# A one-layer hybrid decoder block: max8 rounds spread over the expert loop, and the work of the tail dealt out anew between ACT, DVE, POOL and PE

## What is computed

```python
x = x + merged @ w_o[l]
x = x + moe(rms_norm(x, g_ffn[l]), ...)          # 64 SwiGLU experts, top 8, one shared expert
ple_gate = jax.nn.sigmoid(rms_norm(x, g_ple_in[l]) @ w_ple_gate[l])
x = x + ple_gate * rms_norm(p[l] @ w_ple_proj[l], g_ple_out[l])
```

## Time and profile before

| | |
|---|---|
| median of three executions | 1212.77 us (1207.9 to 1215.7) |
| the profiled execution | 1205.96 us, span 1204.2 us |
| mean granted clock of TensorE in it | 0.989 of full |
| busy: PE, DVE, ACT, POOL | 1142.6 (95%), 840.2 (70%), 771.5 (64%), 398.4 us (33%) |
| bytes moved | 291.52 MB, mean 242 GB/s |
| expert loop, last matmul at | about 1127.8 us |
| projections of `p` | 1133.5 to 1149.4 us |
| gate matmuls | 1152.8 to 1199.6 us |

### The profile page before, as it was taken

How to read it: one execution, slowest core, us unless ns; L and a number is a source line. 1 busy time by engine, 2 the same in 40 slices (tenths; PEclk the granted TensorE clock), 3 DMA queues, 4 the chain that set the end, 5 groups by cost and what they waited for, 6 DMA issues and landing times. The chain is left out here.

```text
span 1204.2 us, 17716 instructions
## 1 busy us (share of the span) xinstructions
PE 1142.6 (95%) x5403; PEld 909.9 (76%) x5403; DVE 840.2 (70%) x1199; ACT 771.5 (64%) x1266; POOL 398.4 (33%) x475
## 2 busy tenths in 40 slices
PE   6999999998999999899999999999999999999898
PEld 5988888697566775688888887777877887777566
DVE  6336432377344336799999998888889998888574
ACT  6534433276233221688888888878888888888471
POOL 1110000042355000155555554445445544453200
PEclk9999999999799999999999999999999999999899
DMA  6312312024001247699999999999999999999611
GB/s 231 141 70 95 114 70 90 20 59 154 37 1 39 102 193 317 238 363 393 384 384 381 382 385 386 357 365 370 355 364 365 364 386 370 368 380 297 189 71 53
DMA packets 71804, 291.52 MB, mean 242 GB/s; under 512 B 15123, under 2 KB 20278, under 8 KB 46806
## 3 DMA queue, kind: packets, MB, share of 16 engines
q1 hardware_dynamic: 52422, 254.15, 54.2%
q0 software_dynamic: 18768, 34.79, 11.4%
q10 hardware_dynamic: 576, 2.10, 0.4%
HBM read 284.61 MB, written 42.07 MB: 271 GB/s over the span
## 5 line engine op out<-in xcount | busy, mean ns | idle before, releaser
L1342 DVE TENSOR_TENSOR arena_r<-arena,win_r 128x1024 fp32r<-128x1024 f32 x256 | 296.5, 1220 | 58.4 <-ACT win_r L905 54.4
L905 ACT ACTIVATE win_r<-arena 128x1024 fp32r<-128x1024 f32 x256 | 250.1, 1056 | 57.5 <-DMA arena<-in_w_exp_up 54.8
L1707 PE MATMUL bank<-win_r,work_r 128*128 128x512 f32 x512 | 206.1, 403 | 21.0 <-DVE x_low_r L1324 18.4
L638 POOL DMA_INDIRECT moe_sum<-ya,sidx x64 | 118.2, 1847 | 254.9 <-ACT ya L933 254.9
L1709 PE MATMUL bank<-arena_r,work_r 128*128 128x512 f32 x512 | 200.8, 392 | 0.0
L1708 PE MATMUL bank<-win_r,x_low_r 128*128 128x512 f32 x512 | 200.3, 391 | 0.0
L1362 DVE TENSOR_TENSOR arena_r<-arena,hT_r 128x1024 fp32r<-128x1024 f32 x128 | 150.4, 1217 | 0.0
L1707 PEld LDWEIGHTS bank<-win_r,work_r 128*128 128x128 f32 x512 | 96.6, 189 | 44.6 <-issue 24.0
L1484 PE MATMUL bank<-arena_r,hT_r 128*128 128x512 f32 (+2 forms) x320 | 120.7, 377 | 0.0
L1485 PE MATMUL bank<-arena_r 128*128 128x512 f32 (+2 forms) x320 | 120.5, 377 | 0.0
L1488 PE MATMUL bank<-win_r,hT_r 128*128 128x512 f32 (+2 forms) x320 | 120.4, 376 | 0.0
(11 more groups left out here) (259 smaller groups left out, 2122.0 us busy)
## 6 DMA issues: line engine op xcount, KB each, us to landing
arena<-in_w_exp_gate SPq DMA_DIRECT2D x64, 1024.0 KB
arena<-in_w_exp_up SPq DMA_DIRECT2D x64, 1024.0 KB
arena<-in_w_exp_down SPq DMA_DIRECT2D x64, 1024.0 KB, 15.3
win<-in_w_in SPq DMA_DIRECT2D x8, 2048.0 KB, 7.8
win<-in_w_o SPq DMA_DIRECT2D x2, 2048.0 KB, 7.7
moe_sum<-resid SPq DMA_DIRECT2D x8, 512.0 KB, 20.1
arena<-in_w_ple_gate SPq DMA_DIRECT2D x2, 2048.0 KB, 17.1
arena<-moe_sum SPq DMA_DIRECT2D x8, 512.0 KB, 7.4
```

The lines of the kernel that those rows point to most:

```text
L638: pool.indirect_dma_start(sums[j % 2], bass.IndirectOffsetOnAxis(sidx[j % 2][0:NS, 0:1], 0), yo[j % 2][0:NS], None, bounds_check=last_toke ...
L905: act.activation(gu_hi[n % 2][:, :, cols], gu_w[n % RING][:, :, cols], ACT.Copy).then_inc(gu_hi_r, 1)
L1342: dve.tensor_tensor(gu_lo[n % RING][:, :, cols], gu_w[n % RING][:, :, cols], gu_hi[n % 2][:, :, cols].bitcast(F32), ALU.subtract).then_inc ...
L1707: pe.matmul(b_, x_hi[:, k, :], w_hi, start=(k == 0), stop=False)
```

## The change

The eight max8 rounds are dealt out one by one to steps 0 to 4 and 61 to 63, each behind the low part of the down weights. In step 63 both halves of the down weights are split ahead of silu (ACT) and of the hidden product (DVE). The two loads of gate weights each wait for their own slot of the ring (`gate_room[c]`), one step earlier than before for the first. `even[t]` is loaded when the even scatters are in, `odd[t]` when the odd ones are. Of the transposes of `p` only the second group waits for `tab_ready`. ACT only squares a projection (`ple_square`), and DVE copies it afterwards (`ple_out`). The high and low parts of the gate weights are cut into pieces between these. The transposes of tile 0 stand ahead of projection 6. The sums of tiles 2 and 3 are made by POOL, behind the last projection.

```diff
--- before.py
+++ after.py
@@ -283,3 +283,3 @@
         xt_done, xt_hi, xt_lo = sem("xt_done"), sem("xt_hi_ready"), sem("xt_lo_ready")
-        gu_hi_r, gu_lo_r, gate_room = sem("gate_up_hi_ready"), sem("gate_up_lo_ready"), sem("gate_room")
+        gu_hi_r, gu_lo_r, gate_room = sem("gate_up_hi_ready"), sem("gate_up_lo_ready"), [sem(f"gate_room{c}") for c in range(2)]
         gu_done, silu_done, a_ready, at_done, at_hi, at_ready = sem("gu_done"), sem("silu_done"), sem("a_ready"), sem("at_done"), sem("at_hi"), sem("at_ready")
@@ -288,3 +288,3 @@
         sum_st, sum_odd_st, pass_ready = sem("sum_started"), sem("sum_odd_started"), sem("pass_ready")
-        x_sum = sem("x_sum")
+        x_sum, x_sum_pool, ple_sq = sem("x_sum"), sem("x_sum_pool"), sem("ple_squared")
         sum_ld = [sem(f"sum_loaded{t}") for t in range(NT)]
@@ -468,4 +468,4 @@
 
-            sp.wait_ge(gate_room, n_pass)
             for c in range(2):
+                sp.wait_ge(gate_room[c], n_pass)
                 sp.dma_start(g_raw[c], a["w_ple_gate"][0][:, c * 512:(c + 1) * 512].rearrange(
@@ -473,6 +473,7 @@
 
-            for i in range(2):
-                sp.wait_ge(scat[i], n_pass * (16 * E // 2))
+            sp.wait_ge(scat[0], n_pass * (16 * E // 2))
             for t in range(NT):
                 sp.dma_start(even[t], sums[0][t * P:(t + 1) * P, :]).then_inc(sum_ld[t], 16)
+            sp.wait_ge(scat[1], n_pass * (16 * E // 2))
+            for t in range(NT):
                 sp.dma_start(odd[:, t, :], sums[1][t * P:(t + 1) * P, :]).then_inc(sum_ld[t], 16)
@@ -665,2 +666,7 @@
 
+            pool.wait_ge(pj_done, P_PLE + 2 * NT)
+            for t in (2, 3):
+                pool.wait_ge(sum_ld[t], 32)
+                pool.tensor_tensor(x[:, t, :], even[t], odd[:, t, :], ALU.add).then_inc(x_sum_pool, 1)
+
 
@@ -839,9 +845,7 @@
 
-            def ple_evac(n):
+            def ple_square(n):
 
-                t, half = divmod(n, 2)
                 act.wait_ge(pj_done, P_PLE + n + 1)
-                b_ = bank[(P_PLE + n) % 4]
-                act.activation(pnb[:, t, half * 512:(half + 1) * 512], b_[:, :], ACT.Copy)
-                act.activation(psq[n % 4], b_[:, :], ACT.Square, accum_out=ssl[:, n:n + 1]).then_inc(pj_free[(P_PLE + n) % 4], 1)
+                act.activation(psq[n % 4], bank[(P_PLE + n) % 4][:, :], ACT.Square,
+                               accum_out=ssl[:, n:n + 1]).then_inc(ple_sq, 1)
 
@@ -897,2 +901,5 @@
                                    ACT.Copy).then_inc(at_hi, 1)
+                    if free and E - 4 <= n < E - 2:
+                        act.wait_ge(gu_done, at(b, q, 1, n + 1))
+                        act.sem_inc(gate_room[n % RING], 1)
                 if not free or 0 <= j + 1 < E:
@@ -909,3 +916,4 @@
                         act.wait_ge(dn_done, at(b, q, 1, j - 1))
-                    act.activation(wdn_hi[j % 2][:, 0, :], wdn[j % RING][:, 0, :], ACT.Copy).then_inc(dn_hi, 1)
+                    for k in range(KF if free and j == E - 1 else 1):
+                        act.activation(wdn_hi[j % 2][:, k, :], wdn[j % RING][:, k, :], ACT.Copy).then_inc(dn_hi, 1)
                     act.wait_ge(gu_done, at(b, q, 1, j + 1))
@@ -919,3 +927,3 @@
                                        ACT.Copy).then_inc(xt_hi, 1)
-                if not free or 0 <= j < E:
+                if not free or 0 <= j < E - 1:
                     act.activation(wdn_hi[j % 2][:, 1, :], wdn[j % RING][:, 1, :], ACT.Copy).then_inc(dn_hi, 1)
@@ -924,5 +932,2 @@
                     act.wait_ge(dn_done, at(b, q, 1, n + 1))
-                    if free and n == E - 4:
-                        act.wait_ge(gu_done, at(b, q, 1, n + 2))
-                        act.sem_inc(gate_room, 1)
                     if not free or n >= 2:
@@ -971,7 +976,10 @@
                 act.activation(pT[:, k, :], bank[4 + T % 2][:, :], ACT.Copy).then_inc(tr_free[T % 2], 1)
-            for n in range(2 * NT):
-                gate_high(0, [n])
-                ple_evac(n)
-            h3_evac(0)
-            gate_high(1, range(KD))
+            highs = [(0, range(0, 4)), (0, range(4, 6)), (0, range(6, 8)), (1, [0]), (1, [1]), (1, [2]), None, (1, [3])]
+            for n, part in enumerate(highs):
+                if part is None:
+                    h3_evac(0)
+                else:
+                    gate_high(*part)
+                ple_square(n)
+            gate_high(1, range(4, KD))
             act.wait_ge(ple_ms, 1)
@@ -980,3 +988,6 @@
             for t in range(NT):
-                act.wait_ge(x_sum, t + 1)
+                if t < 2:
+                    act.wait_ge(x_sum, t + 1)
+                else:
+                    act.wait_ge(x_sum_pool, t - 1)
                 act.activation(h3[t], x[:, t, :], ACT.Square, accum_out=st[0][:, t:t + 1]).then_inc(f_sq, 1)
@@ -1327,2 +1338,10 @@
 
+            def down_low(b, q, j):
+                for k in range(KF):
+                    dve.wait_ge(dn_hi, at(b, q, KF, KF * j + k + 1))
+                    dve.tensor_tensor(wdn_lo[j % RING][:, k, :], wdn[j % RING][:, k, :],
+                                      wdn_hi[j % 2][:, k, :].bitcast(F32), ALU.subtract).then_inc(dn_lo, 1)
+
+            round_steps = [0, 1, 2, 3, 4, E - 3, E - 2, E - 1]
+
             def step(b, q, j):
@@ -1346,5 +1365,4 @@
                 if free and j == E - 1:
-                    tops_of(b, range(0, 4))
+                    down_low(b, q, j)
                 if free and j == E:
-                    tops_of(b, range(4, ROUNDS))
                     lists_of()
@@ -1358,7 +1376,6 @@
                     x_low(b, q, j + 1)
-                if not free or 0 <= j < E:
-                    for k in range(KF):
-                        dve.wait_ge(dn_hi, at(b, q, KF, KF * j + k + 1))
-                        dve.tensor_tensor(wdn_lo[j % RING][:, k, :], wdn[j % RING][:, k, :],
-                                          wdn_hi[j % 2][:, k, :].bitcast(F32), ALU.subtract).then_inc(dn_lo, 1)
+                if not free or 0 <= j < E - 1:
+                    down_low(b, q, j)
+                if free and j in round_steps:
+                    tops_of(b, [round_steps.index(j)])
 
@@ -1379,2 +1396,4 @@
                 if t == 0:
+                    for i in range(4):
+                        dve.wait_ge(pj_free[i], P_PLE // 4 + 2)
                     dve.wait_ge(ple_rt, 1)
@@ -1409,15 +1428,28 @@
 
-            gate_low(0, range(5))
+            def ple_out(n):
+                t, half = divmod(n, 2)
+                dve.wait_ge(ple_sq, n + 1)
+                dve.tensor_copy(pnb[:, t, half * 512:(half + 1) * 512],
+                                bank[(P_PLE + n) % 4][:, :]).then_inc(pj_free[(P_PLE + n) % 4], 1)
+
+            gate_low(0, range(0, 4))
+            ple_out(0)
+            gate_low(0, range(4, 6))
+            ple_out(1)
+            gate_low(0, range(6, KD))
+            ple_out(2)
+            ple_out(3)
             dve.wait_ge(tr_done, T_P + PLE // P)
             add_odd(0)
-            gate_low(0, range(5, KD))
-            dve.wait_ge(pj_free[3], P_PLE // 4 + 2)
-            link(dve.tensor_reduce(st[4], v2(sm, 76, NT, 2), AX.X, ALU.add))
-            mean(st[5], st[4], D, EPS).then_inc(ple_ms, 1)
-            dve.wait_ge(pj_done, P_PLE + 2 * NT)
+            ple_out(4)
+            ple_out(5)
             h3_low(0)
+            ple_out(6)
+            ple_out(7)
+            gate_low(1, range(0, 2))
+            dve.wait_ge(pj_done, P_PLE + 2 * NT)
             add_odd(1)
-            gate_low(1, range(KD))
-            add_odd(2)
-            add_odd(3)
+            gate_low(1, range(2, KD))
+            link(dve.tensor_reduce(st[4], v2(sm, 76, NT, 2), AX.X, ALU.add))
+            mean(st[5], st[4], D, EPS).then_inc(ple_ms, 1)
             dve.wait_ge(f_sq, NT)
@@ -1751,5 +1783,6 @@
 
-            pe.wait_ge(tab_ready, n_pass + 1)
             pe.wait_ge(ld_p, 16)
             for k in range(PLE // P):
+                if k == 1:
+                    pe.wait_ge(tab_ready, n_pass + 1)
                 transposes(T_P + k, [pbuf[:, t, k * P:(k + 1) * P] for t in range(NT)])
@@ -1758,4 +1791,14 @@
             pe.wait_ge(ld_pj, 16)
+            def h3_T(t):
+                if t < 2:
+                    pe.wait_ge(x_sum, t + 1)
+                else:
+                    pe.wait_ge(x_sum_pool, t - 1)
+                for half in range(2):
+                    transposes(T_H3 + 2 * t + half, blocks(x[:, t, :], half))
+
             for n in range(2 * NT):
                 t, half = divmod(n, 2)
+                if n == 6:
+                    h3_T(0)
                 project(P_PLE + n, [(pT[:, k, tok(t)], wpj[:, k, half * 512:(half + 1) * 512])
@@ -1763,8 +1806,2 @@
 
-            def h3_T(t):
-                pe.wait_ge(x_sum, t + 1)
-                for half in range(2):
-                    transposes(T_H3 + 2 * t + half, blocks(x[:, t, :], half))
-
-            h3_T(0)
             for t in range(NT):
```

4 lines of the change are left out of this document (2 added, 2 removed).

## The result

The changed kernel takes 1215.22 us (median of 20 executions), the kernel before 1210.24 us (20 executions measured beside it; the three shown above have 1212.77). One of the changed kernel's 20 took 2924.84 us and is not in the ratio; without it the median is 1214.55. The ratio is **1.0042, 95% interval 1.0025 to 1.0059**: 5.1 us slower (3.0 to 7.1), within the 1% that the prediction called no change. Its profiled execution took 1214.55 us with a span of 1212.8.

The account below looks back on a forecast made before the run. Loop held by PE and DMA; tail gains count only by moving tile 1's start. Tile 1 -0.3, clock +2.5, early rounds +0.3: 2.5 us more on the 1212.77 median, 1215; 8 in 10 range 1206.5 to 1219.

Parts of the forecast that it names:

- the late sum: Projection stage: the sum of token tile 0 comes late behind the last scatter; bounds 0 and 2.3 us, taken as 1.0.
- the clock in the gap: Ahead of tile 1: PE idles 5 us, the granted clock falls to half; 1.7 to 3.4 us lost, taken as 2.5.
- Slot lists and projections: Loop end: slot-list matmul 2.2 us earlier, projections 3.4 us earlier; eight projections in about 14.5 us.
- the last scatter decides: Rival, 15%: the last scatter competes with 2 MB of even loads; sum 2.3 us late, another clock fall, 7.2 us more, 1220.
- POOL and DVE: Second gate half: they exclude each other, so two POOL adds of 2.35 us each cost DVE's low parts 3.5 us.
- The mean behind the low parts: Tail: PLE norm mean follows all eight `gate_low(1)`, ACT's root waits, then 6.95 us to tile 1; 7.1 us gain becomes 0.3.
- Gate loads and down weights: Gate loads slot by slot and last down weights split ahead of silu: nothing on the path, no gain.
- Early rounds: Loop steps 1 to 4: max8 rounds put DVE behind; bounds 0 and 1.5 us, taken as 0.3.
- PE never waits: Rival, 10%: the chain to tile 1 is shorter, clock and sum hold, the whole 7.1 us arrives; 1206.

Follow-up runs that it names:

- e2: Changed kernel with the sums of tiles 2 and 3 on DVE behind the PLE mean, none on POOL; +4.2 us against the kernel before (1.9 to 6.7).
- e3: Changed kernel with the PLE norm's reduce and mean ahead of the second gate half's low parts; +0.5 us against the kernel before (-2.1 to 3.1).
- e1: Changed kernel with both scatters waited for, then even and odd loads in turn, as before; +4.0 us against the kernel before (1.2 to 6.9).
- e5: Changed kernel with its eight max8 rounds back at the loop end; +4.1 us against the kernel before (1.9 to 6.4).
- e4: Changed kernel with sum loads together, all four sums on DVE and the PLE mean ahead of the low parts; ratio 0.9968 against the kernel before.
- e8: The kernel before, unchanged, measured again as if it were a change; ratio 0.9982 (0.9963 to 1.0000).

## Why the prediction was right, and where it was not

The time, 1215.2, is the forecast's 1215, but the change is 5.1 us and not 2.5: the median that I added to, 1212.8 of three executions, was itself 2.5 us above that of twenty. That the number fits to 0.2 us is luck: two errors of some 2.5 us cancel. By the tails alone it is 4.0 us where my sum had 2.2. The direction and the mechanisms were right. In the tail the late sum cost 3.3 us more than I had, the clock in the gap 0.9 less and the rest up to tile 1 0.6 less, 1.8 together.

- **Slot lists and projections: right.** Gain 2.4 us for the slot-list matmul (2.2 forecast), 3.6 for the projections (3.4), and six of them in 10.54 us at full clock. All eight took 19.4 us and not 14.5, as PE's wait and the second fall of the clock lie among them.
- **The late sum: the term that was mis-sized.** I had bounds of 0 and 2.3 us and took 1.0; PE waited 2.62. The scatter took 3.5 us longer beside the even loads. The upper bound was the right reading (and by 0.3 us too low), and the sentence that "a slow transfer at low rate shares well" was wrong. The 35 GB/s that I read for the scatter alone belong to a stage that ends 1.25 us behind its issue; from its issue to 1134.6 the engines moved 54 GB/s. The rival "the last scatter decides", at 15%, described what happened, though its price of 7.2 us was too high: the second fall of the clock gave 1.7 us, not 3.4, and e2 and e3 had the wait without the fall. With 1.6 more of wait and these 1.7, the gate matmuls started 24.0 behind the marker instead of the 20.9 that I had.
- **POOL and DVE: right.** 3.1 us lost on the first two low parts (3.5 forecast), 2.40 and 2.85 us for the POOL sums (2.35 each; the estimate from the Trainium skill's figure was 2.2).
- **The mean behind the low parts: right, and its weight was seen.** ACT's root came behind the mean with its table loaded long before, and from it to tile 1 were 6.7 us (6.95). Tile 1 came 2.4 us later than before, where I had 0.3 earlier; the difference is the late sum and the clock (1.6 and 1.7 us), less what the other terms came out smaller.
- **The clock in the gap: right in kind.** The gap was 4.4 us (5 forecast); from tile 1 to the end took 40.9 us instead of 39.3, so 1.6 and not 2.5. The same gap cost 2.6 us in e1 and 1.7 in e5, and e2's of 3.13 us cost 2.9, so its length does not set the price; e4's of 2.13 us cost nothing.
- **Gate loads and down weights: nothing, as said.** PE takes no wait for either in the tail; neither was tried by itself.
- **Early rounds: 0.3 taken, between 0 and 2.5 left open.** By ACT's copy of the gate product the changed kernel is 0.46 us behind before at expert 0, at most 2.13 on the way to 700 (expert 9), and 0.40 there, as forecast; the 4.76 us by which it is late at expert 59 arise behind that, in steps that are the same in both kernels. That one profile is no proof, as e8's shows.
- **"PE never waits" (1206)** failed by the three waits. e3 shows what it lacked: with one group of two instructions moved, the tail shrank by 8 us.

## What to carry to other kernels

When work is brought forward, look at what it then runs beside: here 2 MB of loads brought forward by 5 us made the transfer that the next loads wait for 3.5 us late, and two sums moved to an idle engine stopped the busy one for 3.1 us. Small instructions on which another engine's chain hangs, as a reduce and a mean of 0.3 us in all, go ahead of the bulk work of their engine: this order was worth 8.0 us here, more than the 7.1 that the change was to gain ahead of the gate matmuls. And compare stretches from an event that both kernels share, since two profiles of one and the same kernel differed by 7 us ahead of it and by 0.1 behind it.
